# A hybrid of two blocks on one core: gates in one pass, and work moved between the stages of the first block

## The chip, the cores and the metric

One core of a Trainium2 chip runs the whole program. The metric is the device time of one execution in microseconds (us); the times shown are the median of three runs and, where the profile is read, that of the one profiled execution. The core has TensorE (PE: matrix products into eight PSUM banks), VectorE (DVE), ScalarE (ACT), GpSimd (POOL) and SyncE (SP, which here only issues DMAs).

## The reference, cut to what matters

256 tokens of width 1024 go through two layers of a first block and then two of a second one, all in float32. A layer of the first block:

```python
h = rmsnorm(x, pre_norm_g[l]); proj = h @ w_in[l]
(u, v, z_a, c_q, c_kv, k_rope, z_b, x_c, z_c, g_a, g_b, g_c) = jnp.split(proj, cuts, axis=-1)
y_a = gmlp_spatial(u, v, ...) * silu(z_a)      # u * (ws_masked @ layernorm(v) + bs)
y_b = mla_attention(c_q, c_kv, k_rope, ...) * silu(z_b)
y_c = rg_lru(x_c, ...) * silu(z_c)             # conv of 4 taps, two sigmoid gates, a linear recurrence over time
merged = sigmoid(g_a) * (y_a @ w_proj_a) + sigmoid(g_b) * (y_b @ w_proj_b) + sigmoid(g_c) * (y_c @ w_proj_c)
x = x + rmsnorm(merged @ w_out[l], post_norm_g[l])
```

The second block has a pooling mixer in its first layer and a sparse attention in its second, and in both a feed-forward part `(silu(g) * a) @ w_down`, where a and g are halves of a product with `w_up` after a convolution of 3 taps, and a gated embedding.

## The kernel before

Activations lie feature by feature: a tile is 128 features by 256 tokens, eight tiles are a tensor of width 1024. Each float32 product is made of three products of a reduced float32 type: ACT rounds a weight piece into `w_hi` (`hi`, L1122), DVE subtracts for the low part `w_lo` (`lo`, L1591), and PE multiplies high by high, high by low and low by high (`three`, L563, L566, L567). Weights come in slots of 1024 x 256 values, each in two pieces of 512 KB; a ring holds six pieces. SP's next load waits until PE has begun on an older piece, and ACT and DVE prepare pieces two slots ahead. A slot gives two output tiles (`features`), 48 products by three of 0.12 us; a round of two slots uses the four PSUM banks called J. The other four banks, K, take the small products.

The work of each engine is a list written out by hand in one fixed order; semaphores tie the lists. In a layer the first block goes through: norm; xc and zc (five rounds, convolution on DVE); the compressed queries and keys (cq, ckv, kr); the gates of the recurrence (L716, 10 tiles, two gates each, banks K; ACT empties them with Sigmoid and then makes Tanh, L1223, L1226); queries (`queries`), their rotation by a product with a swap matrix (L730) and `rotate` on DVE (L1765 to L1770); keys and values (`keys_values`, twice; DVE copies the values to vm, L1787); scores (L744 to L753), softmax; zb; the attention's product with the values; v and its layer norm; u and z_a, four rounds; the spatial product (L809) and its y (`ya_tile`, `low_y` on DVE, cast to ya_hi on ACT); then the squares ga, a, gb, b, gc (two rounds each: a gate's logits, a projection, and so on), c and out.

The recurrence's ten tiles are worked off beside these: `begin` (three instructions on DVE, a reciprocal among them), `root` on ACT (Sqrt), `finish` on DVE (five, a scan over time among them), `high_yc` and `last` (high and low part of the result). Before, tiles 0 to 3 lie in the four rounds of u/za, 4 and 5 in ga, 6 and 7 in a, 8 and 9 in gb. b and gc have none.

A SiLU is made in two steps: ACT writes the Sigmoid of a bank into SBUF (`first_of`), DVE multiplies it by the bank and frees the bank. At z_a a further product by u follows (L1902). An ACT function that isn't in the loaded table costs an ACT_TABLE_LOAD; the compiler places them.

The function `gate` of ACT, as it stands for ga, gb and gc, is

```python
evac("J", 2 * j + n, G[:, dyn(i, 4, 2 * j + n), :], ACT.Sigmoid)
if j == 0 and tile0 is not None:
    root(i, tile0)
```

and G shares its place with wsT, so the spatial product comes ahead of ga.

Of the kernel before, what the change touches and what calls it, by code (L numbers as in the profile page):

```python
# [16 lines left out]
P = 128  # L17
# [25 lines left out]
SW = 256  # L43
# [179 lines left out]
def program(nc, slots, ins, out):  # L223
    ctx = ExitStack()
    with ctx:
# [13 lines left out]
        def kb(n):  # L239
# [33 lines left out]
             ("uz", [P, KT, TOK], F32), ("rec", [P, 1, TOK], F32), kb(4), ("yc_hi", [P, LT, TOK], F32R), ("yc_lo", [P, LT, TOK], F32R)],  # L273
# [77 lines left out]
        def _(sp):  # L351
# [31 lines left out]
            for l in range(L):  # L383
# [164 lines left out]
        def _(pe):  # L548
# [139 lines left out]
            for l in range(L):  # L688
# [123 lines left out]
                square("ga", h)  # L812
# [300 lines left out]
        def _(act):  # L1113
# [67 lines left out]
            for l in range(L):  # L1181
# [3 lines left out]
                for i in range(5):  # L1185
# [1209 lines left out]
```

## Time and profile before

| | |
|---|---|
| median of 3 runs | 1712.76 us (1712.62 to 1718.04) |
| profiled execution | 1711.61 us, span 1709.8 us |
| PE busy | 1553.8 us, 91% |
| PE weight loads | 1504.3 us, 88% |
| DVE busy | 1138.0 us, 67% |
| ACT busy | 880.8 us, 52% |
| mean granted clock of TensorE | 0.957 of full speed |
| moved by DMA | 239.23 MB, 140 GB/s |

The page gives busy time per engine as a share of the span. A busy engine can be at half speed, and an idle one costs nothing unless it is the one that sets the end; for that there is the chain of waits, which follows the last instruction back from releaser to releaser. A time in a row is counted from the start of the span. In a list in order of time a row begins with its start and its duration, and a bracket tells how long the engine stood idle before it and who ended that; "x20" is a merged run of 20.

### The profile page before, as it was taken

What the parts mean: (1) busy time and instruction counts of PE and PEld (TensorE: products, weight loads), DVE (VectorE), ACT (ScalarE), POOL (GpSimd) and SP (SyncE); (2) the same over time, 40 slices, a digit from 0 to 9 for tenths busy, and PEclk for the clock granted to TensorE, in tenths of its full rate; (3) what the DMA queues carried; (4) which work ended last, traced back from release to release, by engine and by line L of the source; (5) the groups of instructions that cost most, each with busy time, mean ns of one, the idle gap of its engine ahead of it and who ended that gap; (6) DMA issues with size and microseconds to landing.
All of it is one profiled execution on the core that took longest, in us unless ns stands there. A gap on an engine that the chain in (4) does not pass through costs nothing.

```text
span 1709.8 us, 28283 instructions
## 1 busy us (share of the span) xinstructions
PE 1553.8 (91%) x11797; PEld 1504.3 (88%) x11797; DVE 1138.0 (67%) x1799; ACT 880.8 (52%) x1564; POOL 88.8 (5%) x141
## 2 busy tenths in 40 slices
PE   4989899799979898997999899999999888899997
PEld 3988899799969888997999789999888777899986
DVE  5653659986667535599866669884676534788755
ACT  3455447564445554475644556653564532566443
POOL 9000000003200000000000100000000000000000
PEclk8999999999999999998999889999899999999998
DMA  4632455466636324563665445555324011455541
GB/s 142 189 94 80 124 173 162 123 185 178 199 89 184 92 83 122 173 172 113 184 203 185 133 131 175 183 174 185 112 89 138 25 50 50 148 179 180 174 159 62
DMA packets 237631, 239.23 MB, mean 140 GB/s; under 512 B 19224, under 2 KB 232274, under 8 KB 237504
## 3 DMA queue, kind: packets, MB, share of 16 engines
q1 hardware_dynamic: 232048, 228.66, 44.0%
q0 software_dynamic: 5456, 8.77, 1.8%
q8 instruction: 94, 1.54, 0.4%
q14 instruction: 33, 0.27, 0.1%
HBM read 236.33 MB, written 1.05 MB: 139 GB/s over the span
## 4 chain that ended last, share of the span: by engine, by line
PE 82%; DVE 7%; ACT 5%; issue 2%; DMA 2%; POOL 1%; DVEq 0%; SPq 0%; POOLq 0%
PE bank L563 24%; PE bank L566 23%; PE bank L567 23%; PE bank L716 2%; PE bank L648 2%; PE bank L1017 1%; DVE rs L1597 1%; ACT w_hi L1122 1%; DVE w_lo L1591 1%; ACT S L1254 1%; PE bank L1003 1%; DMA raw<-in_mla_w_ukv 1%; PE bank L919 1%; DMA raw<-in_w_out 1%; POOL rows L485 1%
## 5 line engine op out<-in xcount | busy, mean ns | idle before, releaser
L563 PE MATMUL bank<-h_hi,w_hi 128*128 128x256 f32 x2344 | 677.4, 289 | 56.7 <-DVE h_lo L1620 23.3
L1591 DVE TENSOR_TENSOR w_lo<-raw,w_hi 128x1024 fp32r<-128x1024 f32 (+1 forms) x460 | 524.6, 1154 | 304.9 <-ACT w_hi L1122 303.5
L566 PE MATMUL bank<-h_lo,w_hi 128*128 128x256 f32 x2344 | 672.6, 287 | 0.0
L567 PE MATMUL bank<-h_hi,w_lo 128*128 128x256 f32 x2344 | 672.2, 287 | 0.0
L1122 ACT CAST w_hi<-raw 128x1024 fp32r<-128x1024 f32 (+1 forms) x460 | 454.1, 990 | 204.4 <-DMA raw<-in_w_in 65.0
L563 PEld LDWEIGHTS bank<-h_hi,w_hi 128*128 128x128 f32 x2344 | 458.3, 196 | 63.4 <-issue 46.3
L566 PEld LDWEIGHTS bank<-h_lo,w_hi 128*128 128x128 f32 x2344 | 458.7, 196 | 0.1
L567 PEld LDWEIGHTS bank<-h_hi,w_lo 128*128 128x128 f32 x2344 | 458.2, 195 | 0.0
L563 PE MATMUL bank<-y_hi,w_hi 128*128 128x256 f32 x352 | 99.7, 283 | 0.0
L567 PE MATMUL bank<-y_hi,w_lo 128*128 128x256 f32 x352 | 99.6, 283 | 0.0
L566 PE MATMUL bank<-y_lo,w_hi 128*128 128x256 f32 x352 | 99.6, 283 | 0.0
L648 PE MATMUL bank<-G,cst 128*128 128x256 f32 x176 | 53.0, 460 | 16.6 <-ACT G L1146 13.8
L566 PEld LDWEIGHTS bank<-y_lo,w_hi 128*128 128x128 f32 x352 | 67.6, 192 | 0.0
L567 PEld LDWEIGHTS bank<-y_hi,w_lo 128*128 128x128 f32 x352 | 67.6, 192 | 0.0
L563 PEld LDWEIGHTS bank<-y_hi,w_hi 128*128 128x128 f32 x352 | 67.6, 192 | 0.0
L648 PEld LDWEIGHTS bank<-G,cst 128*128 128x128 f32 x176 | 37.8, 229 | 29.6 <-issue 17.2
L716 PE MATMUL bank<-xc,wg 128*128 128x256 f32 x208 | 50.7, 408 | 9.7 <-ACT R L1223 9.7
L1127 ACT ACTIVATE G<-bank 128x256 f32<-128x256 f32 x64 | 24.7, 386 | 65.4 <-PE bank L567 65.4
L716 PEld LDWEIGHTS bank<-xc,wg 128*128 128x128 f32 x208 | 42.8, 207 | 17.2 <-ACT R L1223 10.5
L563 PE MATMUL bank<-w_hi,h_hi 128*128 128x256 f32 x176 | 51.6, 293 | 4.3 <-issue 4.3
L566 PE MATMUL bank<-w_lo,h_hi 128*128 128x256 f32 x176 | 51.0, 290 | 0.0
L567 PE MATMUL bank<-w_hi,h_lo 128*128 128x256 f32 x176 | 51.0, 290 | 0.0
(367 smaller groups left out, 2531.8 us busy)
## 6 DMA issues: line engine op xcount, KB each, us to landing
raw<-in_w_in SPq DMA_DIRECT2D x160, 512.0 KB, 3.8
raw<-in_ffn_up SPq DMA_DIRECT2D x88, 512.0 KB, 3.5
raw<-in_ffn_down SPq DMA_DIRECT2D x32, 512.0 KB, 3.4
raw<-in_w_proj_a SPq DMA_DIRECT2D x16, 512.0 KB, 3.4
raw<-in_w_proj_b SPq DMA_DIRECT2D x16, 512.0 KB, 3.4
raw<-in_w_out SPq DMA_DIRECT2D x16, 512.0 KB, 4.5
raw<-in_ple_gate SPq DMA_DIRECT2D x16, 512.0 KB, 3.4
raw<-in_w_proj_c SPq DMA_DIRECT2D x16, 384.0 KB, 3.2
```

The lines of the kernel that those rows point to most:

```text
L485: pool.dma_start(rows[ROW[name]:ROW[name] + n, l, :], src).then_inc(sems["rows_in"], 16)
L563: first = pe.matmul(out_, lh, rh, start=start, stop=False)
L566: pe.matmul(out_, lh, rl, start=False, stop=False)
L567: return pe.matmul(out_, ll, rh, start=False, stop=stop)
L648: mm = pe.matmul(acc(b), c["ones"], sq[:, t, :], start=(t == 0), stop=(t == n - 1))
L716: mm = pe.matmul(acc(b), wg[:, g, rep, pair, :], xc[:, 5 * rep + i_, :], start=(n == 0), stop=(n == len(near) - 1))
L919: mm = pe.matmul(ps[b][:, n:1 + n], w1[:, n, k, :], par[:, ROW2["posv" if n else "posk"] + k:ROW2["posv" if n else "posk"] + k + 1], start ...
L1003: mm = pe.transpose(ps[b][:, n * P:(n + 1) * P], src, c["ident"])
L1017: mm = pe.matmul(o_, pt, vsw[:, k, a, g * HD:(g + 1) * HD], start=k == 0, stop=k == qt)
L1122: act.copy(w_hi[b][:, 0:size], raw[b][:, 0:size]).then_inc(sems["hi_done"], 1)
L1127: ins_ = act.activation(dst, ps[b][0:rows_, 0:width] if src is None else src(ps[b]), func or ACT.Identity, bias=bias, scale=scale)
L1591: dve.tensor_tensor(w_lo[b][:, 0:size], raw[b][:, 0:size], w_hi[b][:, 0:size].bitcast(F32), ALU.subtract).then_inc(sems["w_split"], 1)
```

## The change

- **SiLU in one pass.** For zc, zb and z_a, and in the second block's feed-forward part, ACT computes Silu. For zc and zb it frees the bank itself and DVE's product is gone. For z_a the slots of u and z_a change places, ACT writes Silu(z_a) into m, and DVE makes one product with u's bank in place of two. In the second block one of two products goes.
- **ga in two halves.** The first round of ga goes ahead of the spatial product, the second behind it; ACT's and DVE's work on y_a goes into the second round. wsT and bs move to another place in SBUF.
- **Recurrence tiles.** ga has none, a has 4 and 5, gb 6 and 7, b 8 and 9.
- **Gates of the recurrence.** ACT empties tiles 0 and 1 before the two Sqrt of the compressed norms, and tiles 2 and 3 before the casts of c_hi.
- **Rotations.** PE's four swap products go behind the first `keys_values`; DVE's four `rotate` go behind the two copies to vm of the first slot, and ahead of the next `lo`.

```diff
@@ overlay
-             ("uz", ...), ("rec", [P, 1, TOK], F32), kb(4), ("yc_hi", ...), ("yc_lo", ...)],
+             ("uz", ...), ("rec", [P, 1, TOK], F32), ("wsT", [P, GM_GROUPS, P], F32),
+             ("bs", [P, GM_GROUPS, P], F32), ("yc_hi", ...), ("yc_lo", ...)],
-            [kb(20), ("ws", [P, GM_GROUPS, P], F32), ("wsT", [P, GM_GROUPS, P], F32),
-             ("bs", [P, GM_GROUPS, P], F32)],
+            [kb(20), ("ws", [P, GM_GROUPS, P], F32)],
@@ SP
-                    load(0, rows_of(w_in, l, 0, KT, i * SW + COL_U, SW))
-                    load(1, rows_of(w_in, l, 0, KT, i * SW + COL_ZA, SW))
+                    load(0, rows_of(w_in, l, 0, KT, i * SW + COL_ZA, SW))
+                    load(1, rows_of(w_in, l, 0, KT, i * SW + COL_U, SW))
@@ PE
                     queries(j, 3 * j)
+                w.go("S", 4), w.go("J", 12)
+                ckv = (c_hi[:, 3:5, :], c_lo[:, 3:5, :])
+                keys_values(0, 0, ckv)
                 for j in range(4):
                     b = side()
-                    pe.wait_ge(free[w.bank("J", 3 * j + 2)], w.turn("J", 3 * j + 2) + 1)
+                    pe.wait_ge(free[w.bank("J", 3 * j - 10)], w.turn("J", 3 * j - 10) + 1)
                     filled(pe.matmul(acc(b), c["swap1"], qr[:, j, :], start=True, stop=True), b)
-                w.go("S", 4), w.go("J", 12)
-                ckv = (c_hi[:, 3:5, :], c_lo[:, 3:5, :])
-                for j in range(2):
-                    keys_values(j, 6 * j, ckv)
+                keys_values(1, 6, ckv)
...
+                def half_square(i, act, ready=None):
+                    for j in range(2):
+                        features(j, 2 * j, TWO, act, ready=None if j else ready)
+                    w.go("S", 2), w.go("J", 4)
+                half_square(0, h)
                 pe.wait_ge(sems["wsT_ready"], w.taken("wsT_ready"))
                 pe.wait_ge(sems["vn_ready"], w.taken("vn_ready"))
...
-                square("ga", h)
+                half_square(1, h)
@@ ACT
-                        first_of("J", 2 + n, zc[:, dyn(i, 2, n), :], ACT.Sigmoid)
+                        evac("J", 2 + n, zc[:, dyn(i, 2, n), :], ACT.Silu)
...
-                for k, n in enumerate((QR, KVR)):
-                    b = w.bank("J", 6 + k)
-                    act.wait_ge(full[b], w.turn("J", 6 + k))
-                    act.activation(hf[:, k, :], acc(b), ACT.Sqrt, bias=c["eps"], scale=1.0 / n)\
-                        .then_inc(sems["rstd_c"], w.given("rstd_c"))
-                for t in range(5):
-                    act.wait_ge(sems["cq_f"], w.taken("cq_f"))
-                    act.copy(c_hi[:, t, :], cqv[:, t, :]).then_inc(sems["c_hi_done"], w.given("c_hi_done"))
                 for t in range(LT):
+                    if t == 2:
+                        for k, n in enumerate((QR, KVR)):
+                            b = w.bank("J", 6 + k)
+                            act.wait_ge(full[b], w.turn("J", 6 + k))
+                            act.activation(hf[:, k, :], acc(b), ACT.Sqrt, bias=c["eps"], scale=1.0 / n)\
+                                .then_inc(sems["rstd_c"], w.given("rstd_c"))
+                    if t == 4:
+                        for k in range(5):
+                            act.wait_ge(sems["cq_f"], w.taken("cq_f"))
+                            act.copy(c_hi[:, k, :], cqv[:, k, :]).then_inc(sems["c_hi_done"], w.given("c_hi_done"))
...
-                        first_of("J", 2 * j + n, zb[:, dyn(i, 4, 2 * j + n), :], ACT.Sigmoid)
+                        evac("J", 2 * j + n, zb[:, dyn(i, 4, 2 * j + n), :], ACT.Silu)
...
-                        evac("J", n, uz[:, dyn(i, 2, n), :])
+                        evac("J", n, m[:, dyn(i, 2, n), :], ACT.Silu)
                     root(i, 0)
                     for n in range(2):
                         hi(1, n)
-                        first_of("J", 2 + n, m[:, dyn(i, 2, n), :], ACT.Sigmoid)
...
                 def gate(label, tile0):
                     for i in range(2):
+                        if label == "ga" and i == 1:
+                            high_ya()
...
-                gate("ga", 4)
-                idle("a", 6)
+                gate("ga", None)
+                idle("a", 4)
                 evacuated_all()
-                gate("gb", 8)
-                idle("b")
+                gate("gb", 6)
+                idle("b", 8)
...
-                        act.activation(sg[:, n, :], ug[:, n, :], ACT.Sigmoid)\
+                        act.activation(sg[:, n, :], ug[:, n, :], ACT.Silu)\
@@ DVE
-                        dve.tensor_tensor(zc[:, t, :], zc[:, t, :], acc(b).rearrange("p (a n) -> p a n", a=1),
-                                                  ALU.mult).then_inc(free[w.bank("J", 2 + n)], 1)
...
                     lo(j, 0), lo(j, 1)
-                for j in range(4):
-                    rotate(qr[:, j, :], j)
...
                         dve.tensor_copy(vm[:, t, j * 512:(j + 1) * 512], ps[b][:, :])\
                             .then_inc(free[w.bank("J", 6 * j + 4 + t)], 1)
+                    if j == 0:
+                        for k in range(4):
+                            rotate(qr[:, k, :], k)
                     lo(j, 0), lo(j, 1)
...
-                            dve.tensor_tensor(zb[:, t, :], zb[:, t, :],
-                                                      acc(b).rearrange("p (a n) -> p a n", a=1), ALU.mult)\
-                                                          .then_inc(free[w.bank("J", 2 * j + n)], 1)
...
-                        dve.tensor_tensor(m[:, t, :], m[:, t, :], acc(b).rearrange("p (a n) -> p a n", a=1),
-                                                  ALU.mult).then_inc(free[w.bank("J", 2 + n)], 1)
-                    for n in range(2):
-                        t = dyn(i, 2, n)
-                        dve.wait_ge(free[w.bank("J", 2 + n)], w.turn("J", 2 + n) + 1)
-                        dve.tensor_tensor(uz[:, t, :], uz[:, t, :], m[:, t, :], ALU.mult)
+                        dve.wait_ge(free[w.bank("J", n)], w.turn("J", n) + 1)
+                        dve.wait_ge(full[b], w.turn("J", 2 + n))
+                        dve.tensor_tensor(uz[:, t, :], m[:, t, :], acc(b).rearrange("p (a n) -> p a n", a=1),
+                                          ALU.mult).then_inc(free[w.bank("J", 2 + n)], 1)
...
                 def with_recurrence(label, tile0, evacuate):
                     for i in range(2):
+                        if label == "ga" and i == 1:
+                            all_ya()
...
-                with_recurrence("ga", 4, none)
-                with_recurrence("a", 6, set_merged)
-                with_recurrence("gb", 8, none)
+                with_recurrence("ga", None, none)
+                with_recurrence("a", 4, set_merged)
+                with_recurrence("gb", 6, none)
...
-                with_recurrence("b", None, add_and_wait)
+                with_recurrence("b", 8, add_and_wait)
...
-                        dve.tensor_tensor(sg[:, n, :], sg[:, n, :], ug[:, n, :], ALU.mult)\
-                            .then_inc(sems["dve_step"], w.given("dve_step"))
```

`high_ya` and `all_ya` are the loops over the eight y_a tiles that stood behind the four rounds of u/za on ACT and DVE, unchanged, now as functions.

## Rows read from the trace of the kernel before

**Rows 1.** The page, chain of work that ended last, share of the span by engine.

```profile
PE 82%; DVE 7%; ACT 5%; issue 2%; DMA 2%; POOL 1%; DVEq 0%; SPq 0%; POOLq 0%
```

**Rows 2.** PE's waits: what waited, for whom, total us, times, longest.

```profile
PE bank L809 <- issue: 18.3, 2, 9.4
...
PE bank L716 <- ACT R L1223: 9.7, 2, 4.9
...
PE bank L563 <- DVE zb L1829: 7.1, 2, 3.6
...
PE bank L730 <- ACT qr L1127: 4.4, 2, 2.5
```

**Rows 3.** In order of time: the gates of the recurrence, both layers.

```profile
115.42 1.28 ACT L1214 ACT_TABLE_LOAD   x1
...
115.87 4.48 PE L716 MATMUL bank<-xc,wg 128*128 128x256 f32 x20
...
117.23 1.75 DVE L1746 RECIPROCAL hf<-hf 128x256 f32<-128x256 f32 x1 [1.90 <-ACT hf L1214]
...
122.79 1.76 DVE L1754 TENSOR_TENSOR c_lo<-cqv,c_hi 128x256 fp32r<-128x256 f32 x5
...
125.15 21.19 PE L716 MATMUL bank<-xc,wg 128*128 128x256 f32 x84 [4.79 <-ACT R L1223]
...
584.71 4.48 PE L716 MATMUL bank<-xc,wg 128*128 128x256 f32 x20
...
614.49 0.59 PE L722 MATMUL bank<-kr,cst 128*128 128x256 f32 x2
```

**Rows 4.** Windows: us, busy PE, PEld, DVE, ACT, POOL (records), clock, DMA share, GB/s.

```profile
125.15:130.00 4.85, 4.85 (x11) 3.87 (x12) 0.00 (x0) 2.31 (x6) 0.00 (x0) 0.50 0.01 3
...
318.00:341.00 23.00, 23.00 (x194) 23.00 (x193) 21.75 (x38) 16.79 (x26) 0.00 (x0) 1.00 0.60 182
```

**Rows 5.** In order of time: rotations, second keys_values, first score.

```profile
164.98 0.41 DVE L1765 TENSOR_TENSOR hf<-bank,cst 128x256 f32<-128x256 f32 x1
...
170.02 0.43 DVE L1770 TENSOR_TENSOR qr<-qr,hf 128x256 f32<-128x256 f32 x1
...
174.77 1.04 ACT L1122 CAST w_hi<-raw 128x1024 fp32r<-128x1024 f32 x1 [4.14 <-DMA raw<-in_w_in]
...
180.00 0.67 PE L744 MATMUL bank<-kn,q 128*128 128x256 f32 x2 [0.83 <-issue]
```

**Rows 6.** In order of time: zb, second activation and PE's second round.

```profile
203.65 0.39 ACT L1135 ACTIVATE zb<-bank 128x256 f32<-128x256 f32 x1
...
205.78 0.42 PE L563 MATMUL bank<-h_hi,w_hi 128*128 128x256 f32 x1 [3.56 <-DVE zb L1829]
```

**Rows 7.** In order of time: from the normalised v to y_a's last low part.

```profile
309.71 2.36 DVE L1912 TENSOR_TENSOR vT<-vT,lnb 128x1024 f32<-128x1024 f32 x2
...
312.17 4.79 PE L809 MATMUL bank<-wsT,vT 128*128 128x128 f32 x28 [8.93 <-issue]
...
313.50 0.42 DVE L1921 TENSOR_TENSOR hf<-bank,bs 128x256 f32<-128x256 f32 x1 [1.43 <-PE bank L809]
...
322.64 0.98 DVE L1839 TENSOR_TENSOR ya_lo<-hf,ya_hi 128x256 fp32r<-128x256 f32 x2
```

**Rows 8.** In order of time: half of a (first two), of b, PE at gc.

```profile
343.57 0.42 DVE L1681 TENSOR_TENSOR xc<-xc,I 128x256 f32<-128x256 f32 x1
...
350.47 0.74 DVE L1957 TENSOR_TENSOR m<-G,bank 128x256 f32<-128x256 f32 x2
...
392.92 0.41 DVE L1964 TENSOR_TENSOR hf<-G,bank 128x256 f32<-128x256 f32 x1
...
394.76 1.23 DVE L1591 TENSOR_TENSOR w_lo<-raw,w_hi 128x1024 fp32r<-128x1024 f32 x1
...
410.44 0.36 PE L563 MATMUL bank<-h_hi,w_hi 128*128 128x256 f32 x1 [0.26 <-issue]
```

More of the change, by code:

```diff
@@ L272, in program @@
              ("vT", [P, TT, GM], F32), ("lng", [P, GM], F32), ("lnb", [P, GM], F32),
-             ("uz", [P, KT, TOK], F32), ("rec", [P, 1, TOK], F32), kb(4), ("yc_hi", [P, LT, TOK], F32R), ("yc_lo", [P, LT, TOK], F32R)],
+             ("uz", [P, KT, TOK], F32), ("rec", [P, 1, TOK], F32), ("wsT", [P, GM_GROUPS, P], F32),
+             ("bs", [P, GM_GROUPS, P], F32), ("yc_hi", [P, LT, TOK], F32R), ("yc_lo", [P, LT, TOK], F32R)],
             [kb(20), ("G", [P, KT, TOK], F32), ("ya_hi", [P, KT, TOK], F32R), ("ya_lo", [P, KT, TOK], F32R)],
-            [kb(20), ("ws", [P, GM_GROUPS, P], F32), ("wsT", [P, GM_GROUPS, P], F32),
-             ("bs", [P, GM_GROUPS, P], F32)],
+            [kb(20), ("ws", [P, GM_GROUPS, P], F32)],
             [kb(20), ("tok_in", [P, TT, D], F32), ("rows", [P, 7, P], F32)],
@@ L1306, in _, with high_ya @@
                         hi(1, n)
-                        first_of("J", 2 + n, m[:, dyn(i, 2, n), :], ACT.Sigmoid)
                     high_yc(i, 0)
                     w.go("S", 2), w.go("J", 4)
-                for t in range(KT):
-                    act.wait_ge(sems["y_f"], w.taken("y_f"))
-                    act.copy(ya_hi[:, t, :], hf[:, t % 2, :]).then_inc(sems["y_hi_done"], w.given("y_hi_done"))
-                w.go("K", 8)
+                def high_ya():
+                    for t in range(KT):
+                        act.wait_ge(sems["y_f"], w.taken("y_f"))
+                        act.copy(ya_hi[:, t, :], hf[:, t % 2, :]).then_inc(sems["y_hi_done"], w.given("y_hi_done"))
+                    w.go("K", 8)
                 def gate(label, tile0):
                     for i in range(2):
+                        if label == "ga" and i == 1:
+                            high_ya()
                         for j in range(2):
@@ L1731, in _ @@
                         lo(1, n)
-                    for n in range(2):
-                        dve.wait_ge(sems["act_part"], w.taken("act_part"))
-                        b = w.bank("J", 2 + n)
-                        t = dyn(i, 2, n)
-                        dve.tensor_tensor(zc[:, t, :], zc[:, t, :], acc(b).rearrange("p (a n) -> p a n", a=1),
-                                                  ALU.mult).then_inc(free[w.bank("J", 2 + n)], 1)
                     w.go("S", 2), w.go("J", 4)
@@ L1893, in _ @@
                     for n in range(2):
-                        dve.wait_ge(sems["act_part"], w.taken("act_part"))
                         t = dyn(i, 2, n)
                         b = w.bank("J", 2 + n)
-                        dve.tensor_tensor(m[:, t, :], m[:, t, :], acc(b).rearrange("p (a n) -> p a n", a=1),
-                                                  ALU.mult).then_inc(free[w.bank("J", 2 + n)], 1)
-                    for n in range(2):
-                        t = dyn(i, 2, n)
-                        dve.wait_ge(free[w.bank("J", 2 + n)], w.turn("J", 2 + n) + 1)
-                        dve.tensor_tensor(uz[:, t, :], uz[:, t, :], m[:, t, :], ALU.mult)
+                        dve.wait_ge(free[w.bank("J", n)], w.turn("J", n) + 1)
+                        dve.wait_ge(full[b], w.turn("J", 2 + n))
+                        dve.tensor_tensor(uz[:, t, :], m[:, t, :], acc(b).rearrange("p (a n) -> p a n", a=1),
+                                          ALU.mult).then_inc(free[w.bank("J", 2 + n)], 1)
                     last(dyn(i, 1, 0))
@@ L1927, in ya_tile, with all_ya @@
                         .then_inc(sems["y_f"], w.given("y_f"))
-                ya_tile(0)
-                for t in range(KT):
-                    if t + 1 < KT:
-                        ya_tile(t + 1)
-                    low_y(t, ya_lo, ya_hi)
-                w.go("K", 8)
+                def all_ya():
+                    ya_tile(0)
+                    for t in range(KT):
+                        if t + 1 < KT:
+                            ya_tile(t + 1)
+                        low_y(t, ya_lo, ya_hi)
+                    w.go("K", 8)
                 def with_recurrence(label, tile0, evacuate):
                     for i in range(2):
+                        if label == "ga" and i == 1:
+                            all_ya()
                         if tile0 is not None:
@@ L2078, in ffn @@
                         dve.wait_ge(sems["sg_ready"], w.taken("sg_ready"))
-                        dve.tensor_tensor(sg[:, n, :], sg[:, n, :], ug[:, n, :], ALU.mult)\
-                            .then_inc(sems["dve_step"], w.given("dve_step"))
-                        dve.wait_ge(sems["dve_step"], w.value("dve_step"))
                         dve.tensor_tensor(ua[:, n, :], ua[:, n, :], sg[:, n, :], ALU.mult)\
```

3 lines of the change are left out of this document (removed).

## The prediction, as it was made before the result was known

> **What bounds the kernel now.** I read the page's chain of waits first: it lies on PE for 82%, with DVE 7% and ACT 5% behind it [rows 1]. The diff adds and removes no matrix product, so it can only win back idle time of TensorE, and the half-speed stretches behind such idle time, or add to them. The list of what PE waited for gives the sizes [rows 2]: two waits of about 9 us in front of L809, two of 4.9 in front of L716, two of about 3.6 on DVE's product into zb, two of about 2.2 in front of L730. They stand in the first block, once in each layer; PE's wait for w_lo behind the layer norm's statistics is of the same kind, but the diff leaves it alone. Then I went through PE, DVE and ACT in order of time around each wait of the first layer.
>
> **Gates of the recurrence.** PE issues 104 records of L716 in each layer: 20 from 115.87, then it waits 4.79 us, then 84 from 125.15 until 146.2, 30.3 us in all; in the second layer 584.71 to 614.49, 29.8 us [rows 3]. The first 20 fill the four K banks. Nothing empties them, for ACT does Sqrt, waits for DVE's two reciprocals (1.75 us each) and for cqv, casts c_hi, and comes to the first Sigmoid only then, after another table load. In the 4.85 us behind the wait the granted clock is 0.50, the 1.2 GHz level [rows 4]. At full speed a record takes 4.48 / 20 = 0.22 us, so 104 take 22.5 to 23.
> After the change ACT empties tiles 0 and 1 first. I take it that Silu's table lacks Sigmoid: load from 115.4 to 116.7, the fourth bank filled at 120.2 and emptied at 120.8, Tanh to 121.2, load for Sqrt to 122.5, two Sqrt to 123.3, load to 124.6, tile 2 emptied by 125.4. PE has filled four more banks by 115.9 + 44 x 0.217 = 125.4 and goes on. DVE needs from first reciprocal to last cqv 5.6 us as now (117.23 to 122.79), so to 128.7. ACT casts c_hi from 127.1 to 129.2, then empties tile 4. PE has filled tile 5 at 115.9 + 60 x 0.217 = 128.9 and waits 0.8 us for that bank. Stage: 22.5 + 0.8 = 23.3 us. **Gain 7.0 and 6.5 us.** Upper end 7.8 (no wait). Lower end below nothing, -1.3: the 4.8 us wait stays and the added load (1.28 us) lies on it. I take the value by the count, since all its parts have rows of their own.
> A page bears on the loads: the Trainium skill, "ScalarE: Activation LUTs", section "What ACT_TABLE_LOAD costs", counts 1283 ns for the load and about 1380 ns of drain, 2.66 us for every switch. In [rows 3] the load at 115.42 ends at 116.70, and DVE has the first Sqrt's result at 117.23, 0.53 us later, so no such drain is seen. With the page's figure the three loads ahead of tile 2 would put ACT 4.1 us later, and this stage would give about 3.5 us a layer.
>
> **Rotations of the queries.** PE stood before L730 until ACT had qr of the fourth slot out, then ran the first keys_values partly at half speed, and in the second waited until ACT had passed the cast of 174.77, itself 4.14 us late by a DMA; the scores start at 180.00 [rows 5]. After the change PE goes at 161.0 into keys_values(0), is held to 162.6 and to 164.1 by banks still full of q and qr, ends at 167.5, turns the four qr until 169.3, and runs keys_values(1) to 174.8. Its first call signals 4 us earlier, so the DMA behind the cast of 174.77 lands at about 170.3 and holds nobody. DVE is late next: two copies of vm to 168.3, four rotations to 173.8 (twelve instructions from 164.98 to 170.45 before, 1.37 us each rotation), two w_lo to 176.1, two copies to 177.4, and the scores want all J banks. They start at 177.5 in place of 180.0. **Gain 2.5 us a layer.** Ends: 5.2 (DVE no limit) and -1 (the rotations, now ahead of w_lo, hold back the low parts of zb's first slot and the last copies, and the clock falls in the wait of 2.7 us).
>
> **One-pass gates.** In zb PE waited until 205.78 for DVE, which did w_lo, product, w_lo, product. With Silu out of ACT the banks are free when ACT ends its second activation at 204.04 [rows 6]; the w_lo that PE also wants ends at 203.9. PE starts at 204.2: **gain 1.6 us a layer**; ends 0 and 3.6. A wait of 2.2 us is left, so the clock may fall there as now.
> For xc/zc and the second block's up-projections I count 0 for the products that DVE loses: the list of PE's waits holds nothing from there, because PE is busy without a gap (194 records in 23 us [rows 4], so 96 are 11.5 us, one round) and covers both engines. Without that cover it would be a gain only, 22 rounds of 0.9 us. In u/za DVE loses two products of a round, 0.75 us, under the same cover. The order in which u and z_a are loaded changes addresses and no size; moving wsT and bs changes no instruction.
>
> **First half of ga before the spatial product.** PE ends u/za at 303.24 (312.17 - 8.93) and waits for the normalised v, which DVE completes at 312.07 (309.71 + 2.36); L809 takes 5.6 us more, ga starts at 317.8: 14.5 us [rows 7]. In the second layer the wait is 9.4 us. After the change PE has 11.5 us of ga first, to 314.8, so 312.07 is hidden. The K banks are late next. ACT can cast the last weight piece of this half only after it emptied bank J2, at 314.9: the cast ends at 316.2, w_lo at 317.4, and only then DVE starts all_ya. PE fills four banks by 316.5, then goes at the pace of the y tiles (eight from 313.50 to 323.62, 1.25 each): banks free at 317.9, 318.7, 320.0, 321.2, the last tile done at 321.7. That is 6.9 us on top of ga. **Gain 7.6 us, and 8.1 in the second layer.** y is whole at 327.5, its first use at 333.2. Ends: 11 (products at full clock and no wait) and 4 (another w_lo round and a low clock).
>
> **Recurrence in b.** ga loses its two tiles, a and gb have two as before, b gets two beside its own sums. A half stage of DVE is then: begin, two w_lo, finish 6.9 us (343.57 to 350.47), two sums 1.84 (392.92 to 394.76), two w_lo 2.3 to 2.4, two sums 1.84, last low part 0.3: 13.2 us against PE's 11.5 [rows 8]. PE now reaches gc at 410.2, so b at 387.1; DVE enters b at 389.7. The first half frees its banks 0.6 us before they are wanted; the second frees J1 at 411.15, and PE starts gc at 411.3 in place of 410.44. **Loss 0.9 us a layer.** Ends: 0, and 4.9 (1.7 late in each half, 1.5 for a low clock behind it).
>
> **Sum.** 13.5 + 5.0 + 3.2 + 15.7 - 1.8 = 35.6 us. The profiled execution took 1711.61 us, its span 1709.8; less 35.6 it is 1676.0. The median of the three runs lies 1.15 above that execution, so I predict 1677.2.
>
> **The rivals.**
> A (forecast, 0.65): as above, its own range 1671 to 1684.
> B (0.20), new waits take half of it: the gates wait again at tile 4 for the reciprocals, DVE in b is late by its whole 1.7 us a half, and the waits of 2 to 3 us that stay pull the clock down. For it: 4.85 us at clock 0.50 behind a wait of 4.79. Gates 3.5, rotations 1, zb 1, ga 5.5, b -3: 8 a layer, 16 us, 1697.
> C (0.10), more than forecast: Silu's table serves Sigmoid too, b has no wait, and DVE, lighter by its products, holds PE nowhere. Gates 7.8, rotations 4, zb 2.5, ga 10: 24 a layer, 48.6 us, 1664. Against it: the copies of vm and the cast behind bank J2 have their place in DVE's and ACT's order whatever their load.
> D (0.05), slower: Silu's table holds nothing else that these stages use, so each run of Silu between other functions costs two loads of 1.28 us. There would be some 130 more (40 in xc/zc, 32 in zb, 16 in u/za, 44 in the second block); once 28 of them lie on the path the gain is gone, with 70 it is 1677 + 90 = 1767. Against it: in [rows 3, 5] weight casts and copies are done in the midst of Sqrt and Sigmoid, and the loads stand before Sqrt and Sigmoid alone. Beside it, the Trainium skill, "ScalarE: Activation LUTs", section "Table sets: the hidden batching unit", puts Sigmoid and Tanh in one set and Sqrt in another, does not place Silu, and wants activations batched by set.
> That the change doesn't do what it says is no case of its own: the order on each engine is written out by hand.
>
> **How the numbers follow.** About 0.3% (5 us) is what can be told from no change. A, B and C are faster, D is slower, and B at its bounds may shrink to nothing: faster 0.94, same 0.02, slower 0.04. The range 1667 to 1694 leaves out D, C's far side and B's.
>
> **What would show it.** PE's list without L716, L730 and L809's 9 us; L716 in 23 us at a clock near 1; L809 in 7 us with waits on DVE's hf; a new wait of about 1 us at the start of gc; about 2 us left in zb and before the scores. Wrong would be: table loads in the rounds of the up-projections, more than 3 us at the start of gc, or L716 again with a wait of several us.

## The result, and the profile after

| | before | after |
|---|---|---|
| median of 4 runs | 1715.4 us (1712.62 to 1718.1) | 1673.38 us (1670.48 to 1676.84) |
| profiled execution | 1711.61 us, span 1709.8 | 1674.16 us, span 1672.3 |
| mean granted clock | 0.957 | 0.964 |

The ratio of the times is 0.9762, 95% interval 0.9745 to 0.9779: 2.4% faster. The forecast was 1677.2 us, range 1667 to 1694. The profiled executions lie 37.5 us apart by span; the medians 42.0, because the profiled one of before was on the short side of its runs. Line numbers moved by up to ten, so L809 is now L814 and L730 is L733.

From the page of the changed kernel, busy time and the engine shares of the chain of waits:

```profile
PE 1545.4 (92%) x11797; PEld 1498.0 (90%) x11797; DVE 1105.7 (66%) x1703; ACT 876.0 (52%) x1550; POOL 88.7 (5%) x141
PE 79%; DVE 10%; ACT 5%; DMA 2%; issue 1%; POOL 1%; DVEq 0%; POOLq 0%
```

The same 11797 matmuls; PE is busy 8.4 us less and idle 29.1 us less (span less busy: 156.0 before, 126.9 after). The larger part is waits. PE's waits in the changed kernel (who waited, for whom: us in all, times, the longest), those that answer to [rows 2]:

```profile
PE bank L563 <- DVE w_lo L1600: 6.6, 3, 2.9
PE bank L563 <- issue: 5.7, 7, 3.8
PE bank L814 <- DVE hf L1916: 3.9, 6, 0.9
PE bank L563 <- ACT zb L1132: 3.8, 2, 1.9
PE bank L744 <- DVE vm L1788: 3.7, 2, 2.3
PE bank L563 <- DVE hf L1962: 2.0, 2, 1.0
PE bank L716 <- ACT R L1230: 1.2, 2, 0.6
```

The 18.3 us in front of the spatial product have become 3.9, the 9.7 in front of the gates 1.2; zb waits for ACT, and at 1.9 us each; the swap products wait for nobody, and 2.3 and 1.4 us stand before the scores (L744), where it was 0.8 twice; 1.0 us a layer is new where gc starts (DVE's sum of b, L1962). The row of w_lo holds the two waits of 2.9 us behind the layer norm, as before, and a third one of 0.9 us among the queries.

**Gates.** PE and then ACT in the first layer, in order of time (start, duration, engine, line, operation):

```profile
115.61 13.11 PE L716 MATMUL bank<-xc,wg 128*128 128x256 f32 x60
129.33 9.76 PE L716 MATMUL bank<-xc,wg 128*128 128x256 f32 x44 [0.60 <-ACT R L1230]
```

```profile
115.73 1.28 ACT L1230 ACT_TABLE_LOAD   x1
...
121.02 1.28 ACT L1221 ACT_TABLE_LOAD   x1
122.31 0.84 ACT L1221 ACTIVATE hf<-bank,cst 128x256 f32<-128x256 f32 x2
123.17 1.28 ACT L1230 ACT_TABLE_LOAD   x1
...
128.10 0.80 ACT L1226 CAST c_hi<-cqv 128x256 fp32r<-128x256 f32 x2 [0.38 <-DVE cqv L1751]
128.81 0.47 ACT L1230 ACTIVATE R<-bank,par 128x256 f32<-128x256 f32 x1
```

The load at 115.73 is the one that was assumed: between Silu and Sigmoid a table is fetched. PE runs through 60 records and waits 0.60 us for tile 4's bank (0.8 was forecast). The same stretch by windows (us, busy time and count of PE, PEld, DVE, ACT, POOL, granted clock, DMA share, GB/s), to be set beside [rows 4] with its 0.50:

```profile
125.15:130.00 4.85, 4.25 (x20) 3.43 (x20) 4.82 (x10) 4.47 (x14) 0.00 (x0) 1.00 0.00 0
```

**Rotations and scores**, PE and DVE (beside [rows 5]):

```profile
160.25 1.89 PE L733 MATMUL bank<-qr,cst 128*128 128x256 f32 x8
...
170.09 0.67 PE L744 MATMUL bank<-kn,q 128*128 128x256 f32 x2 [2.34 <-DVE vm L1788]
```

```profile
166.44 2.36 DVE L1600 TENSOR_TENSOR w_lo<-raw,w_hi 128x1024 fp32r<-128x1024 f32 x2
168.71 1.28 DVE L1788 COPY vm<-bank 128x512 f32<-128x512 f32 x2
```

DVE is late next, as forecast: the last rotation ends at 166.5, then come two w_lo and two copies, then the scores. The wait has a price: the scores and what is queued with them took 12.16 us at clock 0.86, where before they took 10.48 at 1.00 (both from windows of that stretch). That is the first layer. In the second the wait is 1.36 us, and the scores take 10.47 us at clock 1.00; the low clock comes later there, in zb.

**zb**, ACT's second activation and PE (beside [rows 6]):

```profile
195.43 0.39 ACT L1132 ACTIVATE zb<-bank 128x256 f32<-128x256 f32 x1
```

```profile
195.92 0.36 PE L563 MATMUL bank<-h_hi,w_hi 128*128 128x256 f32 x1 [1.92 <-ACT zb L1132]
```

The stretch right behind this restart by windows, first layer and second (where PE restarts at 645.86 behind 1.90 us):

```profile
195.92:200.62 4.70, 4.70 (x39) 4.70 (x40) 4.53 (x4) 3.28 (x5) 0.00 (x0) 1.00 0.47 121
645.86:650.56 4.70, 4.70 (x26) 4.70 (x27) 4.53 (x4) 3.28 (x5) 0.00 (x0) 0.64 0.39 112
```

Two waits of the same length, and only the second is followed by a low clock: 26 records in 4.70 us in place of 39.

**v, ga's first half and the spatial product**, DVE and PE (beside [rows 7]):

```profile
297.24 2.36 DVE L1907 TENSOR_TENSOR vT<-vT,lnb 128x1024 f32<-128x1024 f32 x2
299.52 3.49 DVE L1600 TENSOR_TENSOR w_lo<-raw,w_hi 128x1024 fp32r<-128x1024 f32 x3
304.41 1.23 DVE L1600 TENSOR_TENSOR w_lo<-raw,w_hi 128x1024 fp32r<-128x1024 f32 x1 [1.40 <-ACT w_hi L1127]
305.55 0.42 DVE L1916 TENSOR_TENSOR hf<-bank,bs 128x256 f32<-128x256 f32 x1
```

```profile
303.22 1.95 PE L814 MATMUL bank<-wsT,vT 128*128 128x128 f32 x16
306.02 1.50 PE L814 MATMUL bank<-wsT,vT 128*128 128x128 f32 x8 [0.85 <-DVE hf L1916]
308.07 0.71 PE L814 MATMUL bank<-wsT,vT 128*128 128x128 f32 x4 [0.54 <-DVE hf L1916]
309.33 0.71 PE L814 MATMUL bank<-wsT,vT 128*128 128x128 f32 x4 [0.55 <-DVE hf L1916]
```

v is ready at 299.60 and PE comes at 303.22. From there to ga's second half (309.80) it takes 6.58 us; 6.9 were forecast, with the cast behind J2 and its w_lo (304.41) as the cause, and that is what the list shows.

**Start of gc**, DVE and PE (beside [rows 8]):

```profile
391.14 0.42 DVE L1962 TENSOR_TENSOR hf<-G,bank 128x256 f32<-128x256 f32 x1
```

```profile
391.66 0.36 PE L563 MATMUL bank<-h_hi,w_hi 128*128 128x256 f32 x1 [0.99 <-DVE hf L1962]
```

**The ledger.** I cut the span at instructions that both kernels issue on PE; a stage is the time from one to the next. Both layers of the first block, from the two profiles:

| stage of PE | before | after | gain | forecast |
|---|---|---|---|---|
| L716's first record to L722 | 30.31 + 29.78 | 23.32 + 23.32 | 13.5 | 13.5 |
| L722 to the first score | 33.82 + 34.04 | 31.16 + 31.92 | 4.8 | 5.0 |
| first score to the attention's product with the values (zb lies in it) | 42.03 + 43.27 | 40.56 + 40.38 | 4.4 | 3.2 |
| from there to the norm at the layer's end (u/za, spatial, squares, out) | 265.31 + 265.02 | 257.82 + 257.87 | 14.6 | 13.9 |
| second block's feed-forward parts | 202.53 + 210.66 | 199.12 + 208.12 | 6.0 | 0 |
| sparse attention of the second block (no edit) | 207.26 | 211.80 | -4.5 | 0 |
| all others | | | -1.1 | 0 |
| span | 1709.8 | 1672.3 | 37.5 | 35.6 |

Two rows ask for a reason: a gain of 6 us where I had counted nothing, and a loss in a stage without an edit. The table is one profile against one, and stages scatter too; where a row rests on less than the scatter, the experiments say so.

### The profile page after: what moved, and what is told of

Its sections match the earlier page's. It is cut to its first block, busy times and chain, and to the rows that moved or that the text cites. A ratio compares the mean times of both kernels' runs of the same rounds, so it can differ in the third digit from the quotient of the medians.

```text
span 1672.3 us, 28189 instructions
## 1 busy us (share of the span) xinstructions
PE 1545.4 (92%) x11797; PEld 1498.0 (90%) x11797; DVE 1105.7 (66%) x1703; ACT 876.0 (52%) x1550; POOL 88.7 (5%) x141
## 4 chain that ended last, share of the span: by engine, by line
PE 79%; DVE 10%; ACT 5%; DMA 2%; issue 1%; POOL 1%; DVEq 0%; POOLq 0%
PE bank L563 23%; PE bank L566 22%; PE bank L567 22%; PE bank L648 2%; DVE w_lo L1600 2%; PE bank L716 2%; ACT w_hi L1127 1%; PE bank L1022 1%; DVE rs L1606 1%; ACT S L1261 1%; PE bank L1008 1%; DMA raw<-in_ffn_up 1%; DMA raw<-in_mla_w_ukv 1%; DMA raw<-in_w_out 1%; PE bank L924 1%
## 5 line engine op out<-in xcount | busy, mean ns | idle before, releaser
L563 PE MATMUL bank<-h_hi,w_hi 128*128 128x256 f32 x2344 | 676.9, 289 | 51.7 <-DVE h_lo L1629 23.3
L648 PE MATMUL bank<-G,cst 128*128 128x256 f32 x176 | 53.8, 468 | 16.3 <-ACT G L1151 13.7
L1160 ACT CAST h_hi<-hf 128x256 fp32r<-128x256 f32 x64 | 25.9, 405 | 41.8 <-DVE hf L1619 41.8
L1140 ACT ACTIVATE ug<-bank,par 128x256 f32<-128x256 f32 x44 | 24.9, 566 | 42.4 <-PE bank L567 42.4
```

The source lines that it names most:

```text
L563: first = pe.matmul(out_, lh, rh, start=start, stop=False)
L648: mm = pe.matmul(acc(b), c["ones"], sq[:, t, :], start=(t == 0), stop=(t == n - 1))
L1140: act.activation(dst, acc(b), func, bias=bias, scale=scale)\
L1160: act.copy(h_hi[:, t, :], hf[:, t % 2, :]).then_inc(sems["h_hi_done"], w.given("h_hi_done"))
```

## The experiments

Each kernel ran in five rounds against the kernel before, in three groups of four that share a chip and the runs of before. The first group is the first four below (before 1714.01 us). The second is the two kernels with moved recurrence tiles, the changed kernel again and the first edit of the last part (1713.17 us). The third is zb and the last three kernels (1711.79 us). "The stage" is one of the table above, and the changed kernel's second profile (`changed`) is what the stages of the others are set against. First each part of the change was undone by itself.

**The gates' old order.** ACT makes both Sqrt and all five casts ahead of tile 0.

```diff
+                (both Sqrt, then the casts of c_hi: wait cq_f, act.copy(c_hi[:, t, :], ...))
                 for t in range(LT):
-                    if t == 2:
-                        (both Sqrt)
-                    if t == 4:
-                        (the casts of c_hi)
```

> The changed kernel with ACT's old order in the gates of the recurrence: both Sqrt and the five casts of c_hi ahead of the first Sigmoid. Theory (the order of ACT's list holds the K banks full): L716 to L722 takes 30 us again in each layer in place of 23.3, with a wait of 4.8 us and a stretch at half clock behind it; the time rises by 13 us against the changed kernel (1673 to 1686 us), ratio to the kernel before about 0.984. Rival (the stage is shorter because DVE is lighter by its products, the order hardly matters): the rise is under 4 us and no wait above 1 us stands at L716.

Measured: ratio 0.9857 (0.9833 to 0.9881), 1687.94 us. The wait is back:

```profile
PE bank L716 <- ACT R L1228: 9.3, 2, 4.8
```

The stage took 30.03 and 29.75 us against 23.32 twice: 13.1 us, and 13 were expected. Every profile with the new order shows 23.3 in both layers.

**Both halves of ga behind the spatial product.** The recurrence's tiles stay as changed.

```diff
-                half_square(0, h)
                 pe.wait_ge(sems["wsT_ready"], w.taken("wsT_ready"))
...
+                half_square(0, h)
                 half_square(1, h)
@@ ACT and DVE
-                        if label == "ga" and i == 1:
+                        if label == "ga" and i == 0:
```

> The changed kernel with both halves of ga behind the spatial product, and y_a's work on ACT and DVE again ahead of the first half; the recurrence tiles stay where the change put them. Theory (half of ga hides the wait for the normalised v): PE waits 8 to 9.5 us in front of the spatial product, the time rises by 15 to 17 us against the changed kernel (1673 to 1689). Rival (it was moving the two tiles out of ga, and one product less in u/za, that let v be ready sooner): the wait is 4 us or less and the rise under 8 us.

Measured: ratio 0.9853 (0.9829 to 0.9877), 1687.05 us.

```profile
PE bank L813 <- issue: 15.7, 2, 7.8
```

From the attention's product to the norm 264.9 and 265.2 us, against 258.3 and 258.1: 13.8 us in the two layers. That is less than the 15 to 17 expected, for the wait is 7.8 us a layer and not 9.1 as before the change: the other edits took 1.3 us of it a layer. Without the half square this brings nothing, for the stages are as long as before (265.3 and 265.0). All that they gained hangs on the half square.

**Sigmoid and two products in the feed-forward parts alone.**

```diff
-                        act.activation(sg[:, n, :], ug[:, n, :], ACT.Silu)\
+                        act.activation(sg[:, n, :], ug[:, n, :], ACT.Sigmoid)\
@@ DVE
+                        dve.tensor_tensor(sg[:, n, :], sg[:, n, :], ug[:, n, :], ALU.mult)\
+                            .then_inc(sems["dve_step"], w.given("dve_step"))
+                        dve.wait_ge(sems["dve_step"], w.value("dve_step"))
```

> The changed kernel with SiLU in two steps again in the second block's up-projections alone (Sigmoid on ACT, two products on DVE). The prediction counted 0 for this edit. Theory formed after the comparison (DVE's extra product holds up the convolution that frees bank J1, so that PE loses 0.43 us in every second round): the gaps of 0.55 us at every second round come back, ten of them, and the time rises by 4 to 6 us (1673 to 1678). Rival (the cover by PE is whole, and the two profiles differ there only by where the half-clock stretches fell): no gaps and a rise of 0 to 1 us.

Measured: ratio 0.9791 (0.9765 to 0.9816), 1675.38 us. The total, expected to rise by 4 to 6 us, can't tell it from the change (1675.92 us), but the stages can: 201.86 and 210.60 us against 199.19 and 207.88, so 5.4 us, while stages without an edit moved the other way (sparse attention 1.5 us shorter). PE's waits, first this kernel, then the changed one:

```profile
PE bank L563 <- issue: 8.9, 18, 3.8
```

```profile
PE bank L563 <- issue: 5.9, 7, 3.8
```

Eleven more waits stand in the row, and ten of them, of 0.3 us, are in the feed-forward parts, five in each; the changed kernel has none there. This is one of them, DVE and PE of this kernel:

```profile
986.48 1.90 DVE L2068 SCALAR_TENSOR_TENSOR ua<-bank,par,ua 128x255 f32<-128x255 f32 x4
```

```profile
987.91 0.28 PE L567 MATMUL bank<-h_hi,w_lo 128*128 128x256 f32 x1
988.48 0.36 PE L563 MATMUL bank<-h_hi,w_hi 128*128 128x256 f32 x1 [0.29 <-issue]
```

and this is the same place in the kernel before, in the same order:

```profile
1050.30 1.90 DVE L2070 SCALAR_TENSOR_TENSOR ua<-bank,par,ua 128x255 f32<-128x255 f32 x4
```

```profile
1051.75 0.28 PE L567 MATMUL bank<-h_hi,w_lo 128*128 128x256 f32 x1
1052.30 0.36 PE L563 MATMUL bank<-h_hi,w_hi 128*128 128x256 f32 x1 [0.27 <-issue]
```

The convolution of ua frees the bank at 988.38 (986.48 + 1.90), and PE's next matmul, due at 988.03 by the pace of 0.12, begins at 988.48: late by 0.45 us. It is so at every second round (the next at 1012.05), and ten times 0.43 to 0.46 are 4.4 of the 5.4 us. The profile puts these waits down to "issue", for no named event ends them by enough. The other 1 us is spread over the stages and has no row of its own. A stretch of 110 us, windows with the columns as above, this kernel and the changed one:

```profile
990.00:1100.00 110.00, 108.92 (x902) 108.22 (x901) 98.52 (x171) 67.61 (x111) 0.00 (x0) 1.00 0.57 179
```

```profile
990.00:1100.00 110.00, 110.00 (x919) 110.00 (x918) 93.69 (x154) 69.50 (x117) 0.00 (x0) 1.00 0.59 180
```

DVE at 98.5 of 110 us was the engine that just failed to keep PE's pace; at 93.7 it does.

**Swap products and rotations in their old places.**

```diff
-                keys_values(0, 0, ckv)
                 (four swap products)
-                keys_values(1, 6, ckv)
+                for j in range(2):
+                    keys_values(j, 6 * j, ckv)
@@ DVE
+                for j in range(4):
+                    rotate(qr[:, j, :], j)
                 (the loop with the low parts and the copies of vm)
-                    if j == 0:
-                        (the four rotations)
```

> The changed kernel with the rotations of the queries back: PE's four swap products ahead of both keys_values, DVE's four rotations behind the low parts and ahead of the copies to vm. Theory: PE waits 2 us or more for qr again, L722 to the first score takes 34 us in place of 31.2 and 31.9, and the time rises by 3 to 5 us (1673 to 1677), less where the low clock behind the new wait before the scores goes too. Rival (the DMA behind the weight cast sets the scores' start in both orders): the rise is within 1 us.

Measured: ratio 0.9794 (0.9771 to 0.9817), 1677.75 us.

```profile
PE bank L730 <- ACT qr L1132: 4.5, 2, 3.2
```

The wait returns, and L722 to the first score takes 32.0 and 36.3 us, 68.4 in sum, against 62.1 to 65.8 in the nine profiles that have the rotations as changed and the copies of vm where the change left them. But the next stage, with zb in it, is shorter with the old order, 38.9 us twice against 40.6 and 40.5: the scores wait 0.83 us, and neither they nor zb run at a low clock behind it. The two stages sum to 146.1 us against 143.9. Even these 2.2 us are not shown to be the order's. In the second layer PE waited 2.21 us early among the queries, because ACT's weight cast stood 3.50 us for a DMA (1.69 in the changed kernel), and the kernel with ga whole has the same wait with the new order (PE and ACT of this kernel, then PE of the one with ga whole):

```profile
597.02 0.36 PE L563 MATMUL bank<-c_hi,w_hi 128*128 128x256 f32 x1 [2.21 <-issue]
```

```profile
595.80 0.83 ACT L1127 CAST w_hi<-raw 128x768 fp32r<-128x768 f32 x1 [3.50 <-DMA raw<-in_mla_w_uq]
```

```profile
605.43 0.35 PE L563 MATMUL bank<-c_hi,w_hi 128*128 128x256 f32 x1 [2.32 <-issue]
```

Eight of these nine have zb in one pass, and their two stages sum to between 142.8 and 146.7 us, so 146.1 is no outlier. The mechanism is shown, a net gain of the move beside one-pass zb is not.

**The recurrence's tiles as before** (4 and 5 in ga, 6 and 7 in a, 8 and 9 in gb), and in a second kernel **tiles 8 and 9 in gc instead of b**. The first, and the second as far as it differs:

```diff
-                gate("ga", None)
-                idle("a", 4)
+                gate("ga", 4)
+                idle("a", 6)
-                gate("gb", 6)
-                idle("b", 8)
+                gate("gb", 8)
+                idle("b", None)
```

```diff
-                idle("b", 8)
-                gate("gc", None)
+                idle("b", None)
+                gate("gc", 8)
```

> The changed kernel with the recurrence tiles where the kernel before had them (4 and 5 in ga, 6 and 7 in a, 8 and 9 in gb), ga still in two halves. Theory (the tiles had to leave ga, for a tile there puts begin and finish, 4.6 us of DVE, ahead of y_a, which banks K wait for; b's wait of 1 us is the smaller price): the wait at the start of gc goes, saving 0.7 us a layer, the spatial product is 2 to 5 us longer, the time rises by 3 to 8 us against the changed kernel. Rival (y_a has slack in the second half of ga, b's wait is the only effect): the time falls by 1.5 us.

> The changed kernel with tiles 8 and 9 in gc in place of b. Theory (in b DVE needs 13.2 us a half against PE's 11.5, in gc it has the room): PE's wait of 1 us for DVE's hf at the start of gc goes, nothing comes in its place because c asks for tile 9 late, the time falls by 1.5 us (0.7 to 1 us a layer). Rival (c has to wait for the last tile): a new wait on DVE's yc_lo at c, the time is the same or rises.

Measured, the first: ratio 0.9815 (0.9788 to 0.9843), 1683.64 us. With `finish` back in ga, all_ya comes later, and PE stands in the midst of the spatial product:

```profile
302.88 1.95 PE L814 MATMUL bank<-wsT,vT 128*128 128x128 f32 x16
309.15 4.53 PE L814 MATMUL bank<-wsT,vT 128*128 128x128 f32 x16 [4.33 <-DVE hf L1916]
```

From its start to ga's second half 10.45 us against 6.57: 3.9 a layer, 7.7 in the total. Moving the tiles is no edit of its own, but a condition of the half square's gain. The second: ratio 0.9773 (0.9749 to 0.9798), 1675.48 us, the changed kernel's time. The 1 us at the start of gc is gone in both layers, and yet the time from ga's second half to the norm is 0.7 us less in the first layer and 0.6 more in the second, where c now waits 0.95 us for a w_lo. The fall of 1.5 us that was expected did not come: nothing that these runs can tell is to be had between b and gc.

**Sigmoid and a product in zb alone.**

```diff
-                        evac("J", 2 * j + n, zb[:, dyn(i, 4, 2 * j + n), :], ACT.Silu)
+                        first_of("J", 2 * j + n, zb[:, dyn(i, 4, 2 * j + n), :], ACT.Sigmoid)
@@ DVE
+                            (wait for ACT, zb = zb * bank, free the bank)
```

> The changed kernel with zb's SiLU in two steps again (Sigmoid on ACT, DVE multiplies and frees the bank). Theory: PE waits 3.5 us again for DVE's product after zb's first round where 1.9 stand now, and the half-clock stretch behind it comes back in the first layer; the time rises by 3 to 6 us against the changed kernel (ratio to the kernel before 0.979 to 0.980). Rival (the low part of the next weights ends at the same time, so the product costs nothing): the wait stays near 2 us and the time is the same.

Measured: ratio 0.9799 (0.9771 to 0.9827), 1678.77 us.

```profile
PE bank L563 <- DVE zb L1833: 7.1, 2, 3.6
```

The stage is 3.15 and 1.56 us longer, 4.7 in sum; 3.2 was forecast. The wait itself differs by 3.3 us, 1.6 a layer. The other 1.4 is clock, in the first layer alone: in the 4.70 us behind the restart (196.21 with two steps, 195.07 in the changed kernel) the granted clock is 0.64 and 1.00. In the second layer it is low in both kernels, 0.66 and 0.64, which is why the cost there is the wait's 1.6 us only.

**The kernel as changed, again.** No edit.

> The changed kernel itself beside the three others on one chip, as their base: ratio to the kernel before 0.976.

Measured: ratio 0.9770 (0.9747 to 0.9793), 1675.92 us, span 1671.2.

**Two waits that are left, taken away.** First the w_lo behind the layer norm's statistics: both casts and both low parts of u/za's first slot ahead of the squares and of DVE's wait for their sum, and in round 0 `root` and `finish` behind the second pair.

```diff
@@ ACT
+                hi(0, 0), hi(0, 1)
                 (squares of v; in the rounds, hi(0, n) and root(i, 0) in its place only if i)
@@ DVE
+                lo(0, 0), lo(0, 1)
                 (wait for the sum of the squares; lo(0, n) and finish in their place only if i)
+                    if not i:
+                        finish(dyn(i, 1, 0))
```

> The changed kernel with the first two weight pieces of u/za's second round cast by ACT ahead of the layer norm's squares, their low parts on DVE in its wait for ACT's sums, and in the first round root and finish behind the second pair of pieces. Theory (PE's wait of 2.86 us behind the layer norm's statistics, and 1.5 us of half clock behind it, come only from where these two low parts stand in DVE's list): both go, the time falls by 7 to 9 us (1673 to 1665). Rival (ACT's chain of square, Sqrt and table loads sets the banks' release anyway): a wait of 1 to 2 us on ACT stays and the fall is 3 us or less.

Measured: ratio 0.9739 (0.9714 to 0.9763), 1669.66 us, span 1664.0: 6.3 us under the changed kernel beside it, where 7 to 9 were expected. The wait is gone, and from the attention's product to the spatial one it takes 89.0 us in each layer against 92.6 in the first profile of the changed kernel. That is 3.5 us a layer, 7.1 in sum, though the wait itself stood for 2.9 a layer and waits of 0.6 for DVE's uz are new. (In the kernels that leave this place alone and have ga in halves the stretch takes 91.5 to 93.5 us.)

Then the copies of vm: both ahead of the low parts.

```diff
                 (loop with the two copies of vm and, behind the first, the rotations)
+                for j in range(2):
                     lo(j, 0), lo(j, 1)
```

> The changed kernel with DVE's two copies to vm of the second slot ahead of the low parts of zb's first slot. Theory (the scores start late only because two low parts stand ahead of the two copies in DVE's list): PE's wait before the scores, 2.3 and 1.5 us now, falls under 0.7 us and with it the half-clock stretch in the scores; zb's first low parts are wanted 10 us later and are in time. The time falls by 3 to 5 us. Rival (the next thing late is ACT's softmax chain, which starts from the same point): the scores start sooner but zb's second round, released by ACT, starts no sooner, and the fall is under 1 us.

> ln_early and vm_first together. Theory (the two places are 60 us apart and add): 10 to 12 us under the changed kernel, 1663 us, ratio to the kernel before 0.970. Rival (the half-clock stretches only move elsewhere): no better than ln_early, 0.974.

> ln_early, vm_first and tiles 8 and 9 in gc. Theory: the wait on hf at gc's start, 1 us a layer, goes too, so 1 to 2 us under ln_vm. Rival, from tiles_gc (the wait went and the time did not fall): the same as ln_vm.

Measured: the copies alone 0.9760 (0.9733 to 0.9788), 1672.1 us: no difference that the totals can tell, where 3 to 5 us were expected. DVE's vm no longer holds the scores: PE waits 0.83 us there. The two stages from L722 on sum to 141.9 us against 143.9. The three kernels with the copies first have 139.3 to 142.1 there, the eight above 142.8 to 146.7, so an effect of some 2 us is likely, though not shown by the totals. Part of the time goes in PE's waits for ACT's q, 3.6 us in two here against 1.2 in one; they differ between kernels that share this order too. Both edits together: **0.9718 (0.9692 to 0.9744), 1664.24 us**, span 1662.3, the best of all, 9 us under the changed kernel's first median and 12 under its second (on another chip); its slowest run (1667.2) is shorter than any of the changed kernel (1670.48). With tiles 8 and 9 in gc on top (the third kernel): 0.9735 (0.9705 to 0.9765), 1667.59 us, no better, as the rival had it.

**The stage without an edit.** Sparse attention took 207.3 us in the kernel before and 208.9 to 217.1 in the profiles of thirteen runs after it, all of which issue the same instructions there (216.8 and 217.1 with the recurrence's tiles moved, 216.8 with the copies first, 208.9 with ga whole, 209.1 with both last edits). About the same 70 us of it in the kernel before and the changed one, by windows:

```profile
1340.00:1410.00 70.00, 57.81 (x380) 51.93 (x378) 30.78 (x52) 26.02 (x98) 0.00 (x0) 0.90 0.09 31
```

```profile
1302.00:1372.00 70.00, 57.82 (x346) 51.85 (x345) 28.38 (x49) 24.15 (x92) 0.00 (x0) 0.83 0.09 26
```

PE is as busy in both, and does 380 records against 346: the time is lost at the lower clock. Where the half-speed stretches fall there differs from run to run of the same kernel too (211.80 and 212.82 us for the changed one). What sets it stays open: no run held that stage's state fixed, and no edit of this document can be credited or blamed for it.

## Why the prediction was right, and where it was not

- **Gates, 13.5 us: right in mechanism and size.** 13.45 in the ledger, 13.1 by undoing it. The count of loads, tiles and banks held closely: tile 4's bank came late by 0.60 us for 0.8. That Silu's table lacks Sigmoid was assumed and is seen in the load at 115.73.
- **The loads themselves.** The Tanh before the load ends at 121.00, the load runs from 121.02 to 122.30, and the Sqrt starts at 122.31. The Trainium skill, "ScalarE: Activation LUTs", section "What ACT_TABLE_LOAD costs", wants about 1380 ns of drain beside 1283 ns of load. The trace agrees with the 1283 and shows no drain. Rival D is out: the profile has 65 loads for 63 before, with one at the first Silu of xc/zc and of each feed-forward part, as before at the first Sigmoid, and none in the rounds behind it.
- **Rotations, 5.0 us: right for the stage, not shown as a net gain.** L722 to the first score gave 4.8, and the scores start 31.2 us behind L722 for 31.3 forecast. The weak step is what comes behind: the forecast had the wait before the scores and a low clock behind it in the list of ends, and nothing for it in the sum. The wait was 2.34 us, and the scores then lost 1.7 us at clock 0.86. Undone, the part costs 2.2 us over two stages, inside the scatter and no more than what one late DMA took in that run.
- **One-pass gates in zb, 3.2 us: undersized,** 4.4 to 4.7. The wait fell as counted, from 3.56 to 1.92. The clock behind it did fall in the second layer (0.64 over 4.70 us), as I had said it may, and stayed at 1.00 in the first; in the test the surplus is that first layer's clock. In the ledger the scores' low clock eats it there, and the surplus is a shorter low stretch in the second layer (16.3 us from the restart to the attention's product for 17.5).
- **Feed-forward parts, 0: this step failed.** They gave 6.0 us, and 5.4 of it comes back as loss when DVE gets its products again. I had read that PE's list "holds nothing from there". It held the row of 9.2 us in 20 waits put down to issue, which I passed by because it names no engine:

```profile
PE bank L563 <- issue: 9.2, 20, 3.8
```

  The cover was complete in [rows 4], a stretch of the first block, and was taken for the second block too, where it was 0.43 to 0.46 us short at every second round. The text had a bound, a gain of 22 rounds of 0.9 us without any cover, but it entered neither the sum nor the range; about a quarter of it was measured.
- **ga's half, 15.7, less the recurrence in b, 1.8: together 13.9 for 14.6.** The spatial product took 6.58 us for 6.9. The wait at the start of gc is the 0.9 us of the forecast (0.99), in its place; but the kernel without it is no faster, so that it costs 1.8 us is not shown.
- **What made the sum come out.** 35.6 was forecast and 37.5 measured by span, with +6.0 (feed-forward) and -4.5 (a stage that only the clock moved) nearly cancelling. That is luck: neither was in the sum. The median fell by 42.0, for the four runs of before have 1715.4 us where the forecast started from 1712.76; set against this the forecast gain is 6.4 us short. Rival B (waits at tile 4 and in b of several us) did not come; C's Silu table is excluded by the load at 115.73.

## What to carry to other kernels

Read the row "issue" in the engine's list of waits with its count: many short ones at an even distance can be a bank that comes just too late, as here, where taking load off the engine that frees it was worth a little more than their sum. When work is put ahead of a wait, look for what else stands before the freed place on the other engines' lists, and move it in the same edit, as the recurrence's tiles here. Where a kernel's totals scatter by several us, prove an edit by the stage that it touches, and look up first how far that stage scatters in the kernels that leave it alone.

## What the runs showed of the hardware that was not expected

An unedited stage took between 207.3 and 217.1 us with the same instructions, in the two windows shown at clock 0.90 and 0.83; that is more than most edits here are worth. Whether a short wait of PE is followed by a low clock can't be told from its length alone. Waits of 1.90 to 1.92 us in zb were followed by clock 1.00 in one layer and 0.64 in the other. But the profiles with zb in one pass have a pattern. Where PE waited 1.2 to 2.3 us before the scores and then 1.9 in zb, 15 of 16 layers had one stretch at the low clock: either the scores took 12.16 us for 10.47, or zb's second round, with the transposes up to the attention's product, took 16.2 to 16.3 for 14.7, never both. Where the first wait was 0.83 us, 2 of 8 layers had one. No run shows what decides it. Removing a wait of 2.9 us behind the layer norm gave 3.5 us a layer.
